# Expert 1's weights loaded step by step into w_out's place during the last output tile, expert 2's in parts

## The reference

```
mod = c_act @ ada_w[l] + ada_b[l]            # shift1, scale1, gate1, shift2, scale2, gate2
u = x * (1.0 + scale1) + shift1
q, k, v, lru_x, lru_gate, gate_a, gate_b = split(u @ w_in[l])
y = sigmoid(gate_a) * y_a + sigmoid(gate_b) * y_b
x = layer_norm(ALPHA * x + gate1 * (y @ w_out[l]), ln1_g[l], ln1_b[l])
u = x * (1.0 + scale2) + shift2
logits = t @ router_w + router_b             # one group of 4 experts, then its top 2
h = silu(t @ w_gate[e]) * (t @ w_up[e])      # EXPERT_FF = 512
f = sum over the chosen e of weight_e * (h @ w_down[e])
x = layer_norm(ALPHA * x + gate2 * f, ln2_g[l], ln2_b[l])
```

## Time and profile before

| | us |
|---|---|
| median of 3 runs | 752.85 |
| the three runs | 752.85, 748.95, 754.19 |
| the profiled execution, as timed | 748.59 |
| its span in the trace | 746.5 |

### The profile page before, as it was taken

How to read it: one execution, slowest core, us unless ns; L and a number is a source line. 1 busy time by engine, 2 the same in 40 slices (tenths; PEclk the granted TensorE clock), 3 DMA queues, 4 the chain that set the end, 5 groups by cost and what they waited for, 6 DMA issues and landing times.

```text
span 746.5 us, 15550 instructions
## 1 busy us (share of the span) xinstructions
PE 657.4 (88%) x6011; PEld 428.1 (57%) x6012; DVE 341.3 (46%) x660; ACT 230.9 (31%) x479; POOL 100.1 (13%) x185
## 2 busy tenths in 40 slices
PE   4799999998999799999999659899999988999910
PEld 0375666675767577777788445455555544555500
DVE  0265444366788776666756673211111111111117
ACT  0234433558654555554500401011111101111113
POOL 0131000110000000000000013222222221222250
PEclk9999999999999899999999958999999999999965
DMA  9999766293211222123693898999999999991156
GB/s 331 355 315 312 253 226 230 86 327 111 86 57 56 86 86 84 57 67 104 214 422 124 317 419 352 418 417 418 419 420 418 418 422 418 419 417 54 42 134 224
DMA packets 83882, 189.13 MB, mean 253 GB/s; under 512 B 7388, under 2 KB 60092, under 8 KB 68488
## 3 DMA queue, kind: packets, MB, share of 16 engines
q1 hardware_dynamic: 67664, 148.66, 52.6%
q0 software_dynamic: 7376, 32.26, 12.7%
q10 hardware_dynamic: 8808, 7.76, 3.1%
HBM read 174.58 MB, written 14.07 MB: 253 GB/s over the span
## 4 chain that ended last, share of the span: by engine, by line
PE 62%; DMA 14%; DVE 11%; ACT 6%; issue 4%; SPq 2%; POOL 1%; ACTq 0%; DVEq 0%; POOLq 0%
PE psum L1498 15%; DMA wu<-in_moe_w_up_dram 8%; PE psum L1509 8%; PE psum L1300 7%; PE psum L1302 7%; PE psum L1301 7%; DMA ada<-in_ada_w_dram 3%; PE psum L1257 2%; PE psum L1421 2%; PE psum L1422 2%; PE psum L1423 2%; DMA raw<-in_w_in_dram 2%; PE psum L1481 2%; ACT ssb L742 2%; PE psum L1488 1%
## 5 line engine op out<-in xcount | busy, mean ns | idle before, releaser
L1498 PE MATMUL psum<-wg,xs 128*32 128x256 f32 x1280 | 150.7, 388 | 7.2 <-DMA wu<-in_moe_w_up_dram 6.6
L1498 PE MATMUL psum<-wu,xs 128*32 128x256 f32 x1280 | 150.7, 388 | 0.0
L1300 PE MATMUL psum<-uh,whi 128*128 128x512 f32 x336 | 137.5, 409 | 1.3 <-DVE wlo L876 1.3
L1302 PE MATMUL psum<-uh,wlo 128*128 128x512 f32 x336 | 131.1, 390 | 0.0
L1301 PE MATMUL psum<-ul,whi 128*128 128x512 f32 x336 | 131.0, 390 | 0.0
L1498 PEld LDWEIGHTS psum<-wg,xs 128*32 128x32 f32 x1280 | 72.4, 112 | 62.1 <-DMA wu<-in_moe_w_up_dram 8.2
L796 ACT ACTIVATE hsil<-psum 64x256 f32<-64x256 f32 x40 | 15.0, 375 | 229.0 <-PE psum L1498 229.0
L1180 DVE TENSOR_TENSOR h_sb<-psum,hsil 64x256 f32<-64x256 f32 x40 | 17.1, 427 | 148.4 <-ACT hsil L796 148.4
L876 DVE TENSOR_TENSOR wlo<-raw,whi 128x1024 fp32r<-128x1024 f32 x42 | 51.4, 1224 | 70.1 <-ACT whi L621 69.8
L1509 PE MATMUL psum<-wd,hT 128*32 128x256 f32 x1280 | 77.4, 382 | 0.6 <-DVE hT L1186 0.6
L1300 PEld LDWEIGHTS psum<-uh,whi 128*128 128x128 f32 x336 | 63.1, 188 | 22.6 <-issue 7.3
(11 more groups left out here) (251 smaller groups left out, 814.8 us busy)
## 6 DMA issues: line engine op xcount, KB each, us to landing
wg<-in_moe_w_gate_dram SPq DMA_DIRECT2D x32, 1024.0 KB, 12.3
wu<-in_moe_w_up_dram SPq DMA_DIRECT2D x32, 1024.0 KB, 15.0
wd<-in_moe_w_down_dram SPq DMA_DIRECT2D x32, 1024.0 KB
raw<-in_w_in_dram SPq DMA_DIRECT2D x42, 512.0 KB, 3.9
ada<-in_ada_w_dram POOLq DMA_DIRECT2D x16, 1024.0 KB, 6.6
ada<-in_ada_w_dram SPq DMA_DIRECT2D x8, 1024.0 KB, 14.6
y_d<-ysb ACTq DMA_DIRECT2D x160, 32.0 KB
y_d<-zrow POOLq DMA_DIRECT2D x8, 512.0 KB, 6.4
```

What stands on the lines that cost most here:

```text
L1300: mmul(bank[s % 2], h[:, k, :], uh[:, k, :], start=(k == 0), stop=False)
L1302: ins = mmul(bank[s % 2], l[:, k, :], uh[:, k, :], start=False, stop=(k == KT - 1))
L1498: ins = mmul(psum[32 * g:32 * g + 32, 0, 0:256], xs[:, k % 2, k // 2, :], wgu[slot][g // 2][:, k, (g % 2) * 256:(g % 2) * 256 + 256], star ...
```

## The change

Three things change.

1. The steps of the output projection run in the order of a table, `OUT_ORDER`. Tiles 0 and 1 are as before. Then come (2,0), (3,0), (2,1), (3,1), then the rest of tile 2, then the rest of tile 3. The wait for the banks stands before each tile's step 0.
2. Every step of tile 3 counts up a new semaphore, `wo_used`. When it has counted k + 1, `woh[k]` and `wol[k]` are done with. SP loads expert 1's six parts one by one as their places are freed; gate first, then up, then down. DVE waits for `wo_used` = 8 in place of tile 3's `wout_ps`.
3. Expert 2's parts no longer follow the logits. Gate goes right behind iota and gate2c; up waits for `part_ps` 3, `fin_n` 4 and the stores of u2 tiles 0 and 1; down waits for `u2_done` 4 and the store of tile 2. For that each store of u2 has a semaphore of its own. `g1r` and `b1r` now follow expert 2's down part.

```diff
+OUT_ORDER = [(t, k) for t in range(2) for k in range(KT)] + [(2, 0), (3, 0), (2, 1), (3, 1)] + [(t, k) for t in (2, 3) for k in range(2, KT)]
...
-            sp.wait_ge(S["wout_ps"], 2 * NT)
+            def piece(e, slot, m, half):
+                ks = slice(4 * half, 4 * half + 4)
+                sp.dma_start(wgu[slot][m][:, ks, :], (wg_v, wu_v)[m][e][:, ks, :]).then_inc(gu_in[slot][half], 16)
+
+            for m in range(2):
+                for half in range(2):
+                    sp.wait_ge(S["wo_used"], 2 * m + half + 1)
+                    piece(1, 1, m, half)
+            for half in range(2):
+                sp.wait_ge(S["wo_used"], 5 + half)
+                sp.dma_start(wdn[1][:, 2 * half:2 * half + 2, :], wd_v[1][:, half, :, :]).then_inc(dn_in[1], 16)
+            sp.wait_ge(S["wo_used"], KT)
             sp.dma_start(iota[:, :], consts[:, C_IOTA:C_IOTA + 64 + P]).then_inc(iota_in, 16)
...
-            load_gate_up(sp, 1, 1, 0)
-            load_gate_up(sp, 1, 1, 1)
-            load_down(sp, 1, 1)
-
+            for half in range(2):
+                piece(2, 2, 0, half)
+            sp.wait_ge(S["part_ps"], 3)
+            sp.wait_ge(S["fin_n"], NT)
+            for t in range(2):
+                sp.wait_ge(u2_st[t], 16)
+            for half in range(2):
+                piece(2, 2, 1, half)
             sp.wait_ge(S["u2_done"], NT)
-            for q in u2_st:
-                sp.wait_ge(q, 16 * NT // 2)
+            sp.wait_ge(u2_st[2], 16)
+            load_down(sp, 2, 2)
             sp.wait_ge(S["logits_ps"], NT)
             sp.dma_start(g1r[:, :], ln1_g[0].partition_broadcast(P)).then_inc(ln1_in, 16)
             sp.dma_start(b1r[:, :], ln1_b[0].partition_broadcast(P)).then_inc(ln1_in, 16)
-            load_gate_up(sp, 2, 2, 0)
-            load_gate_up(sp, 2, 2, 1)
-            load_down(sp, 2, 2)
...
-            def out_tile(t):
-
-                if t == 1:
-                    pe.wait_ge(S["logit_done"], NU)
-                if t >= 2:
-                    pe.wait_ge(S["fin_n"], t - 1)
-                for k in range(KT):
+            def out_tiles():
+
+                for t, k in OUT_ORDER:
                     if t == 0:
                         pe.wait_ge(S["y_lo"], k + 1)
                         pe.wait_ge(S["split_lo"], NPROJ + k + 1)
-                        if k == 0:
+                    if k == 0:
+                        if t == 0:
                             pe.wait_ge(S["evac"], NPROJ)
+                        elif t == 1:
+                            pe.wait_ge(S["logit_done"], NU)
+                        else:
+                            pe.wait_ge(S["fin_n"], t - 1)
                     for n in range(2):
                         ins = out_product(t, n, k)
-                ins.then_inc(S["wout_ps"], 2)
-
-            for t in range(NT):
-                out_tile(t)
+                    if t == NT - 1:
+                        ins.then_inc(S["wo_used"], 1)
+                    elif k == KT - 1:
+                        ins.then_inc(S["wout_ps"], 2)
```

More of the change, by code:

```diff
@@ L355, in hybrid_layer @@
         ln1_in = sem("ln1_in")
-        u2_st = [sem(f"u2_st{i}") for i in range(2)]
+        u2_st = [sem(f"u2_st{i}") for i in range(NT)]
         y_st = [sem(f"y_st{i}") for i in range(4)]
@@ L364, in hybrid_layer @@
             ya_done sq_done g_arg g_tanh gelu_done yb_done y_done y_hi y_lo ada2_used
-            mod2_raw mod2_row wout_ps ln_sqrt_in ln_sqrt x1_done u2_done u2T_ps u2T_sb part_ps part_sb logits_ps
+            mod2_raw mod2_row wout_ps wo_used ln_sqrt_in ln_sqrt x1_done u2_done u2T_ps u2T_sb part_ps part_sb logits_ps
             rt_exp_in rt_exp m_done pos_ps ctrl_done pool_went pe_went y_zero z_done idx_ready onehots idx_ps slotw wcol_ps
@@ L545, in _ @@
             for q in u2_st:
-                pool.wait_ge(q, 16 * NT // 2)
+                pool.wait_ge(q, 16)
             pool.wait_ge(S["idx_ready"], 1)
@@ L755, in store_u2 @@
                 act.wait_ge(S["u2_done"], t + 1)
-                act.dma_start(u2_d[t * P:(t + 1) * P, :], u2[t][:, :]).then_inc(u2_st[t % 2], 16)
+                act.dma_start(u2_d[t * P:(t + 1) * P, :], u2[t][:, :]).then_inc(u2_st[t], 16)
             def u2_columns(t):
@@ L1050, in _ @@
                 yv, z = psum[:, b0:b0 + 2, :].rearrange("p a n -> p (a n)"), x1[:, t, :]
-                dve.wait_ge(S["wout_ps"], 2 * (t + 1))
+                if t < NT - 1:
+                    dve.wait_ge(S["wout_ps"], 2 * (t + 1))
+                else:
+                    dve.wait_ge(S["wo_used"], KT)
                 if t >= 1:
@@ L1069, in _ @@
             dve.wait_ge(S["logits_ps"], NT)
-            dve.wait_ge(S["wout_ps"], 2 * NT)
+            dve.wait_ge(S["wo_used"], KT)
             lgp = bank[6][:, 0:64].rearrange("p (t e) -> p t e", t=NT)
@@ L1434, in out_tile @@
                         pe.wait_ge(S["split_lo"], NPROJ + k + 1)
-                        if k == 0:
+                    if k == 0:
+                        if t == 0:
                             pe.wait_ge(S["evac"], NPROJ)
+                        elif t == 1:
+                            pe.wait_ge(S["logit_done"], NU)
+                        else:
+                            pe.wait_ge(S["fin_n"], t - 1)
                     for n in range(2):
                         ins = out_product(t, n, k)
-                ins.then_inc(S["wout_ps"], 2)
-            for t in range(NT):
-                out_tile(t)
+                    if t == NT - 1:
+                        ins.then_inc(S["wo_used"], 1)
+                    elif k == KT - 1:
+                        ins.then_inc(S["wout_ps"], 2)
+            out_tiles()
             for t in range(NT):
```

## The result

| | before | after |
|---|---|---|
| median us (20 runs each, same chip) | 751.72 | 748.16 |
| lowest to highest | 748.14 to 755.45 | 742.75 to 752.49 |
| the profiled execution, as timed | 748.59 | 750.24 |
| its span | 746.5 | 748.4 |

The ratio is 0.995, with a 95% interval from 0.9931 to 0.9968: the change saves 3.6 us (2.4 to 5.2).

A forecast was written before the change was run, and what follows sets the result against it. Bound at the hand-over by block 0's gather, queued behind weights on DMA, and later by the weight stream. Terms -2.9 - 0.6 + 0.3 = -3.2 us gave 745.4 against the profiled execution, 749.7 as median; range 745.4 to 753.5.

The forecast's parts named there:

- Nobody waits for experts 1 and 2, the gather does: At the hand-over to the experts: earlier weights give nothing directly; block 0's token-row gather waits behind them on DMA.
- Gather, -2.9 us: Gather of block 0's token rows finds DMA free and lands in 2.85 us in place of 5.75.
- POOL's copy, -0.6 us: POOL's first copy of gathered rows takes 0.4 us in place of 1.01, no longer waiting for DVE at the port.
- The order, +0.3 us: In the output projection PE stops at (3,0) until DVE has read tile 1's banks: 0.3 us lost.
- DMA free with 4 to 6 us in hand: Before the gather at 439.90: 12.3 MB from 404.5 at 419 GB/s end at 433.9, or 436 with small rows.
- The rival that DMA is not free in time: Gather stays at 5.75 us if 4 us more are lost; only the order's 0.3 us left, 753.1 us; chance 0.09.
- The rows g1r and b1r, at nothing: Queued behind SP's new waits, wanted by DVE at 443.3 and landed by 436: no cost.
- Tile 3 covered by 3.2 us: In the output projection, DVE's wait of 3.2 us before tile 3 covers tile 2 ending 2.7 us later.
- Clock, block 0 at 6.2 us: Block 0's products stay at 6.2 us; bounds 2.6 us less at the higher clock, 1.0 us more at the lower.
- the stream is relieved too: Rival in the expert stage: PE's weight waits of 6.6 us go as well, 743.1 us; chance 0.07.
- Slower by (3,0): Rival in the output projection: late x rows stop PE at (3,0); 6 us late is 1.8 us slower, 754.7; chance 0.06.

The follow-up runs named there:

- the natural order: The changed kernel with the output projection's steps in plain order, tile 2 then tile 3; 748.65 us, ratio to the kernel before 0.996.
- the second profile of after: The changed kernel, nothing altered, profiled once more; 750.88 us.
- expert 2 in parts alone: The changed kernel, but expert 1 issued as one load after the last output step, expert 2 in parts behind it; 752.83 us, ratio to the kernel before 1.0012.
- the second profiles: The kernel before and the changed kernel, nothing altered, each profiled once more; 756.77 and 750.88 us.

## Why the prediction was right

It forecast 749.7 us and a step of -3.2 us; the median is 748.16 us, and the step -3.6 (2.4 to 5.2). The traces give -3.5 or -3.6 with +0.25, so -3.3. Of the 1.5 us between forecast and median, 1.1 us is the starting point: the kernel before is at 751.72 by 20 runs and was at 752.85 by three.

- **Nobody waits for experts 1 and 2, the gather does.** Right by the traces. Undoing half of the change left the gather at 4.18 us or about 6, and the medians were 749.91 and 752.83 us. By their times alone these two runs can't settle it, as their intervals hold 1.000. What settles it is that PE waits for no weights before 518.98 us in the kernel before, and that the gather takes 2.82 us too where expert 2 comes later than before.
- **Gather, -2.9 us.** Right in the profile of before (5.75 to 2.85). Its usual size is larger: with a full DMA it took 5.75, 6.06, 6.11 and 6.40 us in four profiles, so -3.2 is typical.
- **POOL's copy, -0.6 us.** The sum with the gather held (-3.5 expected, -3.5 and -3.6 measured), the split did not. The first copy of before took 1.01 us only in that profile. The port's price was 0.6, 0.3 and 0 us in three profiles, about 0.3 on average. When the gather lands 0.6 us later, DVE's instruction is all but over and the copy takes 0.40 us. The Trainium skill (SBUF — State Buffer, Who interferes with whom) makes the copy wait for a DVE instruction that holds the shared port, and the rows agree: 1.01, 0.70 and 1.26 us where one ran, each time ending 0.26 us behind it, and 0.40 us where none did or only for 0.09 us.
- **The order, +0.3 us.** Right: 0.25 us in two profiles of after, and gone in the natural order. In one of them x came 0.5 us too late on top of it; the kernel before would have absorbed that (it had 9 us in hand), the changed one doesn't.
- **DMA free with 4 to 6 us in hand.** Too good, and this is the step that failed without harm. I counted 12.3 MB at 419 GB/s and 2 us for the small rows, 31.4 us from 404.5 on. In the profile of after it began at 407.1 us (34 GB/s from 404 to 408), but the gather was later by the same 2.6 us. What was mis-sized is the length: 12.8 MB at 382 GB/s, 33.5 us, to 440.6. There were 1.9 us in hand (442.52 - 440.6), 3.4 in the second profile of after, whose gather came later behind tile 3, and about 1 in the natural order. The rival that DMA is not free in time deserved more than 0.09.
- **The rows g1r and b1r, at nothing.** Right in time, wrong in its number: b1r landed at 442.1 us (issued 425.46, 16.6 us later), not by 436, and DVE wanted it at 445.97. With expert 2 in parts alone this became a stall of 9.3 us.
- **Tile 3 covered by 3.2 us.** Right, nearly used up: DVE waits 0.49 us there after, 3.19 before.
- **Clock, block 0 at 6.2 us.** Right: 6.24. In the second profiles it is 5.54 us before and 5.62 after.
- **The stream.** SP issues expert 3 at 453.65 us, 39.7 us behind tile 3, against 43.2 before (454.50 - 411.35): the same 3.5 us. PE's waits for weights are 5.6 and 6.0 us in two profiles of after, 6.6 and 5.8 of before. The waits didn't go, so that the stream is relieved too is refuted.
- **Slower by (3,0).** Not in the ordinary kernel, but the mechanism is real, and dearer than priced: 6 us of lateness were to make it 1.8 us slower than before; about 6 us made it 4.4 (0.6%). The stall was the 5 us that the prediction has; the lower clock behind it, 1.6 us, was missing in its sum.

## What to carry to other kernels

A bulk load for which nobody waits can still cost time through the small transfer that shares its DMA engines. Its best place is a stretch where DMA is idle and the buffer is freed piece by piece; put behind the small transfer instead, it cost about 9 us here. Before a wait is moved forward in an in-order stream, look for what feeds it late: 9 us of slack became 1 us, and a stall costs more than its length when it takes the clock down with it.

## What the runs showed of the hardware

- A gather of 128 rows of 1 KB landed in 2.8 to 2.9 us when DMA was idle, in 4.2 us when DMA ran empty about 1 us before the landing, and in 5.7 to 6.4 us when it was full throughout. It is the same transfer; what differs is what is queued beside it.
- A 0.5 MB row issued behind 12 MB of weights landed 25.9 us later (expert 2 in parts alone), 16.6 us in the kernel after, and 8.0 before.
- A stall of PE of 5.0 us was followed by the granted clock of 0.51 for 3 us, which cost 1.6 us more.
- A POOL copy that met a DVE instruction with two SBUF inputs ended 0.26 us behind that instruction, and the profile counts the wait into the copy's own length (0.40 us alone; 0.70, 1.01 and 1.26 us so).
- PE pauses 2.4 to 4.7 us after block 3 in every profile, for nothing that the profile shows. Its cause is open.
- Two executions of one kernel differed by 8.2 us as timed (748.59 and 756.77). A single profile shows mechanisms, not the size of a 0.5% change.
